# Both ends of the up stage in another order, and mixed tokens from heads and rests, in a two-layer decoder trunk

## The reference

```python
x = layer_norm(ALPHA * x + mixer(x), ln_mix_g[i], ln_mix_b[i])
x = layer_norm(ALPHA * x + conv_ffn(x, ...), ln_ffn_g[i], ln_ffn_b[i])

def conv_ffn(h, w_up, conv_w, conv_b, w_down):
    u = h @ w_up                      # (512, 1024) @ (1024, 5632)
    up = jnp.pad(u, ((0, 0), (CONV_WIDTH - 1, 0), (0, 0)))
    c = conv_b
    for j in range(CONV_WIDTH):
        c = c + conv_w[j] * up[:, j:j + S]
    g, val = c[..., :FFN_DIM], c[..., FFN_DIM:]
    return (jax.nn.silu(g) * val) @ w_down   # (512, 2816) @ (2816, 1024)
```

## Time and profile before

| | |
|---|---|
| median of three runs | 1231.78 us (1230.88 to 1231.8) |
| the profiled execution's own time | 1231.07 us |
| its span, first to last instruction | 1229.3 us |
| PE busy | 1191.5 us, 97% |
| DVE, ACT, POOL busy | 735.9, 628.5, 678.7 us |
| mean granted clock of TensorE | 0.995 |
| up stage, layer 0 and layer 1 | from 272 and from 862 us, to 506 and to 1096 us |

### The profile page before, as it was taken

How to read it: one execution, slowest core, us unless ns; L and a number is a source line. 1 busy time by engine, 2 the same in 40 slices (tenths; PEclk the granted TensorE clock), 3 DMA queues, 4 the chain that set the end, 5 groups by cost and what they waited for, 6 DMA issues and landing times.

```text
span 1229.3 us, 20284 instructions
## 1 busy us (share of the span) xinstructions
PE 1191.5 (97%) x7714; PEld 1052.3 (86%) x7714; DVE 735.9 (60%) x1368; ACT 628.5 (51%) x1089; POOL 678.7 (55%) x418
## 2 busy tenths in 40 slices
PE   9999999998999999899999999999899999999997
PEld 9877777787999999888888788878899999987885
DVE  2045656358988888612280355654999888872126
ACT  3245555445766666512342466753566666652223
POOL 4543535255877777655534333334577777765453
PEclk9999999999999999999999999999999999999999
DMA  7321212131233323322232212122123222232311
GB/s 290 112 86 61 91 63 94 36 104 35 103 107 107 111 107 110 128 97 89 103 109 99 78 60 68 69 69 103 35 93 114 103 103 103 102 137 103 102 68 69
DMA packets 20041, 117.44 MB, mean 96 GB/s; under 512 B 2448, under 2 KB 2832, under 8 KB 7568
## 3 DMA queue, kind: packets, MB, share of 16 engines
q1 hardware_dynamic: 18400, 112.21, 25.8%
q10 hardware_dynamic: 1584, 4.51, 1.1%
HBM read 110.41 MB, written 2.10 MB: 92 GB/s over the span
## 4 chain that ended last, share of the span: by engine, by line
PE 82%; DVE 8%; ACT 4%; POOL 3%; issue 2%; DVEq 0%; ACTq 0%; POOLq 0%
PE bank L1480 32%; PE bank L1181 28%; PE bank L1212 13%; POOL w_lo L302 2%; PE bank L1264 2%; PE bank L1291 1%; PE bank L1350 1%; PE bank L1329 1%; ACT w_hi L400 1%; PE bank L1278 1%; DVE x L824 1%; DVE a_lo L1115 1%; PE bank L1156 1%; DVE ln_mul L801 1%; PE bank L1339 1%
## 5 line engine op out<-in xcount | busy, mean ns | idle before, releaser
L302 POOL TENSOR_TENSOR w_lo<-w_raw,w_hi 128x1024 fp32r<-128x1024 f32 x116 | 297.2, 2584 | 370.0 <-ACT w_hi L400 359.8
L400 ACT ACTIVATE w_hi<-w_raw 128x2048 fp32r<-128x2048 f32 x55 | 105.2, 1912 | 208.7 <-PE bank L1181 200.7
L1480 PE MATMUL bank<-t_hi,w_hi 128*128 128x256 f32 x640 | 181.4, 283 | 2.9 <-POOL w_lo L361 2.9
L1480 PE MATMUL bank<-t_hi,w_lo 128*128 128x256 f32 x640 | 181.1, 283 | 0.0
L1480 PE MATMUL bank<-t_lo,w_hi 128*128 128x256 f32 x640 | 181.1, 283 | 0.0
L361 POOL TENSOR_TENSOR w_lo<-w_raw,w_hi 128x512 fp32r<-128x512 f32 x120 | 156.9, 1308 | 20.6 <-ACT w_hi L612 19.8
L1181 PE MATMUL bank<-w_hi,a_hi 128*128 128x512 f32 x480 | 153.3, 394 | 9.6 <-DVE a_lo L1115 6.8
L1181 PE MATMUL bank<-w_hi,a_lo 128*128 128x512 f32 x480 | 152.0, 391 | 0.0
L1181 PE MATMUL bank<-w_lo,a_hi 128*128 128x512 f32 x480 | 151.7, 391 | 0.0
L1212 PE MATMUL bank<-xt_hi,w_hi 128*128 128x512 f32 (+1 forms) x416 | 148.1, 356 | 2.4 <-ACT v_all L430 1.7
L1212 PE MATMUL bank<-xt_lo,w_hi 128*128 128x512 f32 (+1 forms) x416 | 148.5, 357 | 0.0
(11 more groups left out here) (129 smaller groups left out, 2518.6 us busy)
## 6 DMA issues: line engine op xcount, KB each, us to landing
w_raw<-w_stream SPq DMA_DIRECT2D x97, 1024.0 KB, 4.8
x<-x_in SPq DMA_DIRECT2D x4, 512.0 KB, 7.5
gain<-ln_in ACTq DMA_DIRECT2D x4, 512.0 KB, 4.1
shift<-ln_in ACTq DMA_DIRECT2D x4, 512.0 KB, 5.1
qs<-qc SPq DMA_DIRECT2D x16, 128.0 KB, 2.0
ks<-kc SPq DMA_DIRECT2D x16, 128.0 KB, 2.0
out<-x SPq DMA_DIRECT2D x3, 512.0 KB, 2.6
w_raw<-w_stream SPq DMA_DIRECT2D x2, 512.0 KB, 6.3
```

Of the source, the lines that this page charges most:

```text
L302: pool.tensor_tensor(w_lo[slot(c)][:, part], w_raw[s][:, part], w_hi[slot(c)][:, part].bitcast(F32), ALU.subtract).then_inc(lo_ready, 1)
L400: act.activation(w_hi[slot(c)][:, :], w_raw[c % 2][:, :], ACT.Copy).then_inc(hi_ready, 2)
L1480: mm = pe.matmul(out, lhs[s][:, at], rhs[:, k, :], start=(k, v) == (0, 0), stop=(k, v) == (3, 2))
```

## The change

Five edits, in both layers:

1. `token_sum` and `x_raw` go. VectorE's `tokens_mixed` adds or subtracts `xt_hi` and then `xt_lo`, each in a step of its own: six instructions for each of the two token tiles instead of four, two of which (`t1` minus `xt_lo`, `t4` plus `xt_lo`) have both inputs in SBUF.
2. ScalarE loads the table of Silu and makes the head of W11 of the first scheme chunk between the heads of x's tile 2 and tile 3; GpSimd makes its rest first of all in the stage.
3. VectorE's `first_sums` of the first scheme chunk stands right behind `tokens_mixed`, ahead of the rests of T1 and T2.
4. At the end, ScalarE makes `a_hi` of down chunks 0 and 1 each behind one half of the weights' heads, makes the heads of the second weight chunk before the last gate, and issues the loads of gain and shift behind that gate.
5. VectorE makes `a_lo` of down chunk 0 before it combines the last values.

```diff
-                token_sum(0)
-                token_sum(1)
+                w_rest(0, W11, w_raw[(b + AT_UP + FIRST) % 2][:, 0:Q])
                 for j in range(2):
                     t_rest(T3, j, 4 * j + 1)
                     t_rest(T4, j, 4 * j + 4)
...
-                            act.wait_ge(raw_full[(b + AT_UP + FIRST + c) % 2], filled(b + AT_UP + FIRST + c, it))
-                            w_head(W11, raw[:, 0:Q])
+                            if not first:
+                                act.wait_ge(raw_full[(b + AT_UP + FIRST + c) % 2], filled(b + AT_UP + FIRST + c, it))
+                                w_head(W11, raw[:, 0:Q])
...
-                        act.preload_act_table(ACT.Silu)
...
                             act.activation(w_hi[slot(down_first)][:, part], w_raw[down_first % 2][:, part],
                                            ACT.Copy).then_inc(hi_ready, 1)
-                        chunk_heads(0, used=False)
+                            chunk_heads(g, used=False)
                         value_combined(last, 1)
+                        act.wait_ge(w_used, down_first)
+                        heads(down_first + 1, used=False)
+                        gate_combined(last, 1)
                         act.wait_ge(*w.at("lo_p", 5 * NW))
                         load_gain(i)
-                        gate_combined(last, 1)
                         silu(KF - 1, 1)
-                        act.wait_ge(w_used, down_first)
-                        heads(down_first + 1, used=False)
...
-                        chunk_heads(1, used=False)
...
                         xt_heads(i + 1, 2)
+                        if i % 2 == 0:
+                            act.preload_act_table(ACT.Silu)
+                            first = after + FIRST
+                            s, part = operand(l, W11)
+                            act.wait_ge(raw_full[first % 2], filled(first, 0))
+                            act.wait_ge(w_used, after)
+                            act.activation(w_hi[s][:, part], w_raw[first % 2][:, 0:Q], ACT.Copy).then_inc(w["hi"], 1)
                         xt_heads(i + 1, 3)
...
-                    dve.wait_ge(*w.at("x", j + 1))
-                    dve.tensor_tensor(t_raw[:, T1, :, part], low, x_raw[:, j, 0:4, :],
-                                      ALU.subtract).then_inc(w["ts"], 1)
-                    dve.wait_ge(*w.at("ts", 4 * j + 2))
-                    dve.tensor_tensor(high, t_raw[:, T1, :, part], high, ALU.subtract).then_inc(w["ts"], 1)
-                    dve.wait_ge(*w.at("ts", 4 * j + 3))
-                    dve.tensor_tensor(t_raw[:, T4, :, part], x_raw[:, j, 4:8, :], high, ALU.add).then_inc(w["ts"], 1)
+                    t1, t4 = t_raw[:, T1, :, part], t_raw[:, T4, :, part]
+                    dve.tensor_tensor(t1, low, xt_hi[:, 0:4, part].bitcast(F32), ALU.subtract).then_inc(w["ts"], 1)
+                    dve.wait_ge(*w.at("ts", 6 * j + 2))
+                    dve.tensor_tensor(t1, t1, xt_lo[:, 0:4, part].bitcast(F32), ALU.subtract).then_inc(w["ts"], 1)
+                    dve.wait_ge(*w.at("ts", 6 * j + 3))
+                    dve.tensor_tensor(high, t1, high, ALU.subtract).then_inc(w["ts"], 1)
+                    dve.wait_ge(*w.at("ts", 6 * j + 4))
+                    dve.tensor_tensor(t4, high, xt_hi[:, 4:8, part].bitcast(F32), ALU.add).then_inc(w["ts"], 1)
+                    dve.wait_ge(*w.at("ts", 6 * j + 5))
+                    dve.tensor_tensor(t4, t4, xt_lo[:, 4:8, part].bitcast(F32), ALU.add).then_inc(w["ts"], 1)
...
                 tokens_mixed(0)
                 tokens_mixed(1)
+                first_sums(0, 0, 0, False)
...
                 early_products(last)
+                chunk_rests(0)
                 values_combined(last, 1)
-                chunk_rests(0)
                 value_taps(KF - 1, 1)
```

More of the change, by code:

```diff
@@ L142, in build @@
         with ExitStack() as st:
-            sb("below_x_raw", [P, KF - 4, S], stack=st)
-            x_raw = sb("x_raw", [P, 2, KD, P], stack=st)
-        with ExitStack() as st:
             sb("below_ln", [P, KF, S], stack=st)
@@ L198, in build @@
         class Half(Phase):
-            each = {"x": 2, "tc": 2, "ts": 8, "th": 8, "tl_v": 4, "tl_p": 4, "a6": NW, "qs": 2 * NW, "s": 2 * NW, "hi": 7 * NW,
+            each = {"tc": 2, "ts": 12, "th": 8, "tl_v": 4, "tl_p": 4, "a6": NW, "qs": 2 * NW, "s": 2 * NW, "hi": 7 * NW,
                     "lo_p": 5 * NW, "lo_v": 2 * NW, "p": 6 * NW, "cp": NW, "cb": 5 * NW, "g_mm": FIRST, "cg": KF, "cv": KF, "g1": KF, "gc": KF,
@@ L344, in _ @@
                 w, u = W[l], U[l]
[L346 to L349, removed]
                 def t_rest(row, j, seen):
@@ L377, in _ @@
                     raw = w_raw[(b + AT_UP + FIRST + m) % 2]
-                    w_rest(m, W11, raw[:, 0:Q])
+                    if m:
+                        w_rest(m, W11, raw[:, 0:Q])
                     w_rest(m, SUM_Q, qs_raw[m % 2][:, 0, :])
@@ L689, in _ @@
                             high = bank[5 + 2 * j][:, :].rearrange("p (k q) -> p k q", k=4)
[L690 to L693, removed]
+                            t_head(T3, j, t_raw[:, T3, :, part], 6 * j + 1)
+                            t_head(T2, j, high, 6 * j + 6)
+                            t_head(T1, j, t_raw[:, T1, :, part], 6 * j + 6)
+                            t_head(T4, j, t_raw[:, T4, :, part], 6 * j + 6)
                         act.wait_ge(*u.at("g_mm", 1))
@@ L1101, in up_body @@
                         w_rest(n, SUM_4, bank[7])
-                    first_sums(m, c, it, level > 1)
+                    if level > 0:
+                        first_sums(m, c, it, level > 1)
                     second_sum(m, c)
```

## The result

| | before | changed |
|---|---|---|
| median | 1231.39 us, 4 runs (1230.88 to 1231.8) | 1217.37 us, 4 runs (1216.62 to 1218.99) |
| profiled execution, its span | 1231.07, 1229.3 us | 1217.66, 1215.9 us |
| ratio, 95% interval | | 0.9888 (0.9871 to 0.9905), 13.8 us less (11.7 to 15.9) |

The forecast was 1219.5 us in 1216.5 to 1224. To see where the difference lies, cut both traces at events that they share: the turn of x's tile 2 ahead of each mixer and up stage, and the start of product SUM_2 in each layer.

A forecast was written before the change was run, and what follows sets the result against it. TensorE was busy 1191.5 of 1229.3 us, so savings had to come from its 38 us of waiting or from lowered clock. Top 5.8 plus bottom 6.2 made 12.0 us less: 1219.5 us, range 1216.5 to 1224.

The forecast's parts named there:

- (a): Top of up stage: without token sums L815 falls to 0.16 and L824 to 1.28 us; 4.20 us saved in layer 0.
- (b): Top: without TensorE's wait the last turn's eight transposes run at full clock; 0.94 us less in layer 0, 0.65 in layer 1.
- (c): Top: the table load moves from before the copies of t_raw into ScalarE's idle stretch; 1.18 us less.
- (d): Top: six VectorE mixing instructions per token half instead of four; four times 0.72, 2.9 us more.
- (e): Top: mixing steps reading only SBUF may wait for GpSimd's port; none at half 0, 0.9 us more at half 1.
- Rival A: Top: GpSimd gets the port at half 0's first SBUF-only subtract; 2.8 us lost in all, 1222.3 us; chance 0.12.
- (g): Top: VectorE's two rests of T1 wait less for GpSimd, 1.15 us and none; 0.45 us less.
- Rival B: Top: three waits in 7 us lower TensorE's clock, costing 3.2 us for both layers; 1222.7 us; chance 0.08.
- Bottom: End of up stage: TensorE's two waits for a_lo shrink, gaining 1.6 and 1.5 us; 3.1 a layer, 6.2 in all.
- Rival C: Bottom gives only half, because the second rests of both chunks become the bound; 1222.5 us; chance 0.10.
- Rival D: Up bodies: a shifted phase makes VectorE the bound, 0.4 us times 36 bodies, 14 us lost; 1234 us; chance 0.05.
- Rival E: Top gives nothing, as token sums were not what blocked L815 and L824; only the bottom gains, 1225 us; chance 0.05.

The follow-up runs named there:

- e5: Changed kernel with GpSimd again doing both token sums at their old place, their results unread; 1227.44 us.
- e9: Changed kernel with Silu's table load put back between the last heads of x and the copies of t_raw; 1222.11 us.
- e3: Changed kernel with the old order put back at the bottom of the up stage; 1223.51 us.
- e6: Changed kernel with write-only GpSimd memsets at the old place of the token sums; 1217.08 us.
- e10: Changed kernel with first_sums of the first body put back behind the taps; 1220.08 us.
- e11: Kernel before with the bottom's order changed for down chunk 0 alone (a_hi 0 and a_lo 0 early); 1234.08 us.
- e1: Kernel before with only the token sums removed and VectorE mixing in six instructions a half; 1226.70 us.
- e2: Kernel before with one added wait: GpSimd holds its token sums until the last norm is done, four-step mix kept; 1223.17 us.
- e7: Changed kernel, but the token sums stay on GpSimd, held until the last norm is done, with the old four-step mix; 1213.30 us.
- e4: Kernel before with the changed order at the bottom alone; 1225.34 us.

## Why the prediction was right

The time and the mechanism held; by its steps:

- **(a), (b), (c).** The mix of tokens was forecast for 284.67 and began at 285.03 - 0.33 = 284.70. L815 at 0.16, L824 at 1.28, the turn at full clock and the table load in ScalarE's idle stretch came as worked out. e5 shows the cause of (a); that of (c) is in e9, with a second job of the table load that the forecast did not have.
- **(d).** Four more steps of 0.69 to 0.72: right.
- **(e), Rival A.** The race at half 0 was called 0.11 us close and measured 0.10, for VectorE. Half 1's last step took 1.46, a wait of 0.77 against 0.9. The rival called the race at half 0 open; it fell the same way in every trace that has it.
- **(g) was mis-sized.** The forecast had the first T1 rest wait 1.15 and the second not at all, 0.45 saved. VectorE got there 0.02 us ahead of GpSimd's T4 rest: 0.68 and 1.18, a wait of 0.5, 0.6 us more saved in each layer. With (e) and small gaps this is the 0.8 to 0.9 us a layer by which the top beat the forecast; the race at half 0 fell to VectorE as forecast, and one that the forecast did not see did too. That this error went the way of the gain was luck: with GpSimd 0.03 us sooner, VectorE would have waited for it there.
- **Three new waits.** Forecast 1.1 to 1.7 us each and under 6 a layer: gaps of 1.18, 1.07, 1.62 in both layers, 3.9 us together, or 3.0 by the waits' rows (0.90, 0.79, 1.34). The forecast had 4 to 5.
- **Rival B, the clock.** It stayed at 1.00. More than that, it is the other way round: the three short waits left it at 1.00 in both layers of the changed kernel, e3 and e6, and one wait of their sum lowered it in both layers of e10. The Trainium skill ("TensorE: Matmul & The Clock Gate", "A second HAM failure mode: psum-queue depth-cycling") has frequent small pauses make the clock swing; pauses of 0.8 to 1.3 us, three in 7, did not here.
- **Bottom, Rival C.** 3.16 and 3.09 against 3.1. Both second rests came a little late, as forecast: the step that needs the first of them starts after 0.59 us instead of 0.46. But the forecast treated the gaps as two gains of 1.6 and 1.5. e11 shows that the first alone is worth nothing; the pair is 3.1.
- **Rival D.** No body became longer; VectorE still has its 0.87 us of idleness in each.
- **Rival E.** Refuted by e1 and e5.

What the forecast left out: that edit 1's benefit was to be had without its cost. Its term (d), 2.9 us a layer, is the price of removing the sums where moving them was enough (e2, e7).

## What to carry to other kernels

When one engine's small instruction suddenly takes as long as another engine's large one, compare their ends, and then move the large one into a stretch where the first engine reads PSUM, before you rewrite the computation to remove it. Price a gap by what the waiting engine needs next: an operand that hangs on a chain of its own comes at an absolute time, so that closing the gap ahead of it only makes the next one longer. Several short waits can be cheaper than one of their sum, since the clock can fall behind the long one; look at the granted clock behind every wait of over 1.5 us, and ask whether the next wait hides what the fall costs.

## What the runs showed of the hardware that was not expected

- The granted clock fell from 1.00 to 0.50 (2.4 to 1.2 GHz) at waits of 4.2 to 4.3 us (before, e4, e5, e11), 3.23 (e10, both layers), 2.8 (e11, both layers), 2.27 (e2, layer 1) and 2.15 (e9, layer 1), but not at 2.26 (e2, layer 0), 2.16 (e9, layer 0), nor at 2.86 and 1.40 in e1. In the changed kernel it also fell once at a wait of only 1.68 us, in the mixer of layer 0; the same wait, 1.65 to 1.68 us, left it at 1.00 in the traces of the other thirteen kernels:

```profile
212.53 1.94 PE L1281 MATMUL bank<-ident,probs 128*128 128x128 f32 x8 [1.68 <-DVE probs_t L877]
...
214.00:216.00 2.00, 2.00 (x19) 1.67 (x19) 0.89 (x2) 0.60 (x1) 0.00 (x0) 0.52 0.34 139
```

- So between 1.7 and 2.9 us the outcome was not settled by the length of the wait alone; what else decides it stays open. A fall cost 1.2 to 1.6 us where work followed it (e10, e2, e11), and nothing where later waits had room for it (e4 above; in e9 SUM_2 starts 30.83 us after the turn of tile 2 in layer 0, without a fall, and 30.85 in layer 1, with one).
- A GpSimd memset of 128x1024 (0.93 us each) runs beside VectorE's two-input instructions without holding them.
- Three races for the port were won by whoever was 0.02 to 0.10 us ahead, and the loser waited for the whole of the other's instruction. In back-to-back GpSimd instructions a waiting VectorE instruction gets in between them (498.94 above), so that it waits for one, not for the pair.
- The table load of 1.28 us was followed by the next ScalarE instruction 0.01 us after its end:

```profile
279.18 1.28 ACT L749 ACT_TABLE_LOAD   x1
280.47 0.63 ACT L754 ACTIVATE w_hi<-w_raw 128x512 fp32r<-128x512 f32 x1
```
